# The last quarter of an MLP input product by seven block products instead of eight, on one Trainium2 core

## The reference, cut to what matters

```python
def reference(x, ...):
    h = rms_norm(x, pre_norm_mix)
    y = hybrid_mixer(h, w_in, ..., w_branch_att, w_branch_dn, w_out)
    x = x + rms_norm(y, post_norm_mix)
    h = rms_norm(x, pre_norm_mlp)
    y = jnp.square(jax.nn.relu(h @ w_mlp_in)) @ w_mlp_out    # 1024 x 4096, 4096 x 1024
    x = x + rms_norm(y, post_norm_mlp)
```

## Time and profile before

| | |
|---|---|
| median of 3 runs | 748.72 us (748.64 to 749.12) |
| the profiled execution | 748.65 us |
| its span | 747.1 us |
| TensorE (PE) busy | 739.8 us, 99% |
| VectorE, ScalarE, GpSimd busy | 436.2, 389.3, 317.3 us |
| MLP input stretch, from its first full unit | 424.68 to 588.37 us |
| MLP output stretch | 588.37 to 741.1 us |

### The profile page before, as it was taken

The page is one execution under the profiler, slowest core; times in us unless marked ns, Lnnn a source line. Parts: engine busy times, 40 slices in busy tenths (PEclk is TensorE's granted clock), DMA queues, the critical chain, the costliest instruction groups (busy, mean ns, idle before and its releaser), DMA issues.

```text
span 747.1 us, 11902 instructions
## 1 busy us (share of the span) xinstructions
PE 739.8 (99%) x4168; PEld 608.1 (81%) x4168; DVE 436.2 (58%) x651; ACT 389.3 (52%) x632; POOL 317.3 (42%) x296
## 2 busy tenths in 40 slices
PE   9999999999999999999999999999999999999996
PEld 7788778888887878788888988888888888888885
DVE  5896899990444545345974511221221777778795
ACT  6657842268555365635655733332332655565671
POOL 2357894535444754574526454645645000000002
PEclk9999999999999999999999999999999999999999
DMA  9336223446365577266651279789877476654752
GB/s 341 102 93 205 57 77 108 127 128 184 113 156 157 192 174 204 60 159 204 207 183 29 84 244 290 186 269 282 231 238 212 159 222 197 197 186 153 219 174 113
DMA packets 52893, 129.21 MB, mean 173 GB/s; under 512 B 6096, under 2 KB 6512, under 8 KB 50544
## 3 DMA queue, kind: packets, MB, share of 16 engines
q1 hardware_dynamic: 49120, 109.47, 44.7%
q0 software_dynamic: 3392, 18.88, 13.1%
q10 hardware_dynamic: 336, 0.28, 0.1%
HBM read 126.49 MB, written 39.86 MB: 223 GB/s over the span
## 4 chain that ended last, share of the span: by engine, by line
PE 93%; POOL 3%; ACT 2%; DVE 1%; issue 0%; POOLq 0%; ACTq 0%; DVEq 0%
PE bank L758 28%; PE bank L760 27%; PE bank L759 27%; POOL rsq L2158 2%; PE bank L1005 1%; PE bank L1028 1%; PE bank L1015 1%; POOL w_lo L2164 1%; PE bank L969 1%; PE bank L779 1%; PE bank L933 1%; PE bank L785 1%; PE bank L980 1%; PE bank L1037 1%; PE bank L788 0%; PE bank L1067 0%
## 5 line engine op out<-in xcount | busy, mean ns | idle before, releaser
L2164 POOL TENSOR_TENSOR w_lo<-raw,w_hi 128x512 fp32r<-128x512 f32 x169 | 220.0, 1311 | 238.4 <-ACT w_hi L1220 236.6
L1220 ACT ACTIVATE w_hi<-raw 128x512 fp32r<-128x512 f32 (+2 forms) x214 | 144.9, 684 | 156.3 <-PE bank L760 122.6
L758 PE MATMUL bank<-h_hi,w_hi 128*128 128x512 f32 (+1 forms) x528 | 208.5, 395 | 0.2
L759 PE MATMUL bank<-h_lo,w_hi 128*128 128x512 f32 (+1 forms) x528 | 204.2, 387 | 0.0
L760 PE MATMUL bank<-h_hi,w_lo 128*128 128x512 f32 (+1 forms) x528 | 204.1, 387 | 0.0
L758 PEld LDWEIGHTS bank<-h_hi,w_hi 128*128 128x128 f32 x528 | 99.1, 188 | 25.5 <-issue 5.1
L760 PEld LDWEIGHTS bank<-h_hi,w_lo 128*128 128x128 f32 x528 | 99.2, 188 | 20.6
L759 PEld LDWEIGHTS bank<-h_lo,w_hi 128*128 128x128 f32 x528 | 99.3, 188 | 18.7
L1629 DVE SCALAR_TENSOR_TENSOR relu_sb<-bank,rs_row 128x512 f32<-128x512 f32 x32 | 20.6, 686 | 126.0 <-PE bank L760 114.3
L2305 POOL TENSOR_SCALAR ssh<-ssy 128x1 f32<-128x1 f32 x4 | 1.0, 238 | 151.6 <-ACT junk L1600 151.6
L758 PE MATMUL bank<-w_hi,a_hi 128*128 128x512 f32 x120 | 46.8, 390 | 0.0
(11 more groups left out here) (327 smaller groups left out, 1260.8 us busy)
## 6 DMA issues: line engine op xcount, KB each, us to landing
raw<-in_w_in SPq DMA_DIRECT2D x87, 256.0 KB, 2.7
raw<-in_w_mlp_in SPq DMA_DIRECT2D x62, 256.0 KB, 5.1
t_sum<-in_w_mlp_out POOLq DMA_DIRECT2D x12, 1024.0 KB, 9.0
raw<-in_w_mlp_out SPq DMA_DIRECT2D x26, 256.0 KB, 2.7
raw<-t_sum SPq DMA_DIRECT2D x26, 256.0 KB, 2.9
v_sum<-in_w_mlp_out POOLq DMA_DIRECT2D x4, 1024.0 KB, 9.4
raw_b<-in_w_mlp_out SPq DMA_DIRECT2D x16, 256.0 KB, 2.9
raw_b<-t_sum SPq DMA_DIRECT2D x14, 256.0 KB, 2.9
```

Of the source, the lines that this page charges most:

```text
L758: pe.matmul(o, s_hi, m_hi, start=start, stop=False, skip_group_check=True)
L759: pe.matmul(o, s_hi, m_lo, start=False, stop=False, skip_group_check=True)
L1220: return a.activation(o, i_, ACT.Copy, scale=scale)
L2164: g.tensor_tensor(w_lo[:, slot, :], raw[:, slot, :], w_hi[:, slot, :].bitcast(F32), ALU.subtract).then_inc(lo_ready, 1)
```

## The change

The first 12 groups (G_PLAIN) of the MLP input stay. The last four, 1024 features, become a product of 2 x 2 x 2 blocks: two halves of the tokens (256), of the rows (512) and of the features (512). It is done in 2 steps (STEPS_IN) of 256 features of each half, and a step has seven products, q1, q6, q5, q2, q7, q3, q4, of two units each (PER_STEP = 14), so 28 units in place of 16. A unit of a product has 12 matmuls of 256 columns. q1, q2 and q4 read w_mlp_in, the other four read sums of its blocks, made in DRAM by copy and add in the attention stage (`IN_SUM_AT`).

The other operands are blocks of h or differences of them, `ts_hi` and `ts_lo`; VectorE makes these in groups 4 to 7 (`full_block`, `t_blocks_made`, `t_low`), ScalarE rounds them. Results are put together from three pairs of banks by VectorE (`step_in`: e1, f, c11, c22, c12, c21, then relu), with one copy of q1 by ScalarE (p1).

In the steps loads go through a ring of 8 slots: four new ones, `raw_m`, and the four of `raw`. Low halves are made by GpSimd for 4 units of a step (LOW_POOL) and by VectorE for the other 10.

The sums of w_mlp_out move. Two more pieces, (0,2) and (1,2), are made ahead of the MLP input, at units 114 and 118. `SUM_IN` is left with seven, in groups 2 to 8, and the piece (3,3) goes into the second step. A copy of q = 3 now always waits for all four adds of t2.

As the blocks of h need room, x_res is copied to DRAM in groups 2 and 3 and read back by GpSimd in the MLP output; pn_mlp is loaded there too, in another place. Slots 6 and 7 of the MLP output (`raw_c`) lie at 84 KB in place of 0, so their first load comes before the others' and not after the MLP input.

```diff
-OUT_SUM_AT = {48: 0, 52: 1, 60: 2, 87: 3}
+OUT_SUM_AT = {55: 0, 61: 1, 70: 2, 85: 3}
-SUM_AT = {61: (0, 0), 65: (1, 0), 73: (2, 0), 74: (0, 1), 78: (1, 1), 86: (2, 1)}
+SUM_AT = {64: (0, 0), 73: (1, 0), 76: (2, 0), 79: (0, 1), 82: (1, 1), 88: (2, 1), 114: (0, 2), 118: (1, 2)}
+IN_SUM_AT = {48: (0, 0), 51: (1, 0), 58: (2, 0), 68: (3, 0)}
-SUM_IN = {2: (0, 2), 3: (0, 3), 4: (3, 0), 5: (3, 1), 7: (2, 2), 8: (2, 3), 9: (1, 2), 10: (1, 3), 12: (3, 2), 13: (3, 3)}
+SUM_IN = {2: (0, 3), 3: (1, 3), 4: (2, 2), 5: (2, 3), 6: (3, 0), 7: (3, 1), 8: (3, 2)}
+IN_PRODUCTS = ("q1", "q6", "q5", "q2", "q7", "q3", "q4")
+LOW_POOL = (1, 3, 7, 11)
...
# SP, MLP input
-        for g in range(2, 16):
+        for g in range(2, G_PLAIN):
             for j in range(4):
                 load(0, j, mlp_source(g, j), g * 4 + (U_OUT + j - RAW - 1))
+                if g in (2, 3) and j % 2:
+                    t = 2 * (g - 2) + j // 2
+                    if t == 0:
+                        sp_.wait_ge(*x2_signal(2))
+                        sp_.wait_ge(*x2_signal(3))
+                    sp_.dma_start(x2_copy[t], x_res[:, t, :]).then_inc(copied_out, 16)
             if g in SUM_IN:
                 q, i = SUM_IN[g]
                 if q == 2:
-                    sp_.wait_ge(t_added[0], 16 * N_SUM)
+                    sp_.wait_ge(*added(0, N_SUM))
                 if q == 3:
-                    sp_.wait_ge(t_added[2], 16 * (2 if i < 2 else N_SUM))
+                    sp_.wait_ge(*added(2, N_SUM))
                 sp_.dma_start(*t_copy(q, i)).then_inc(t_copied[q], 16)
+        for s in range(STEPS_IN):
+            for v in range(PER_STEP):
+                u = U_S + PER_STEP * s + v
+                if v >= RING - RAW or s:
+                    sp_.wait_ge(*low_of(u - RING))
+                sp_.dma_start(raw_of(u), in_source(s, v)).then_inc(raw_signal(u)[0], 16)
+                if (s, v) == (1, 0):
+                    sp_.wait_ge(*added(3, 3))
+                    sp_.dma_start(*t_copy(3, 3)).then_inc(t_copied[3], 16)
...
# TensorE, one product of a step (waits for banks left out)
+            for half in range(2):
+                u = U_S + PER_STEP * s + 2 * IN_PRODUCTS.index(name) + half
+                pe.wait_ge(*low_of(u))
+                for kk in range(2):
+                    for e in range(2):
+                        c = slice(kk * 256 + e * P, kk * 256 + e * P + P)
+                        x_ = three(bank[IN_BANK[name] + e][:, 0:256], w_hi[:, u % SPL, c], w_lo[:, u % SPL, c],
+                                   *in_operand(name, 2 * half + kk), name in ("q1", "q6", "q5") and half + kk == 0,
+                                   name in ("q2", "q4", "q3") and half + kk == 2)
+                x_.then_inc(unit_done, 1)
...
# SP, MLP output
-        for s in (4, 5, 0, 1, 2, 3):
+        sp_.wait_ge(unit_done, U_M1 - PER_STEP + 4)
+        for s in (4, 5, 6, 7, 0, 1, 2, 3):
...
# GpSimd, MLP input
-        for u in range(U_OUT + 6, U_M1):
+        def add_sum(q, i):
+            g.wait_ge(*copied(q, i + 1))
+            g.dma_start(*t_add(q, i), accum_op=ALU.add, max_dma_last_dim=8192).then_inc(t_added[q], 16)
+
+        for u in range(U_OUT + 6, U_S):
             split_u(u)
             if (u - U_OUT) % 4 == 1 and (u - U_OUT) // 4 - 1 in SUM_IN:
-                q, i = SUM_IN[(u - U_OUT) // 4 - 1]
-                g.wait_ge(t_copied[q], 16 * (i + 1))
-                g.dma_start(*t_add(q, i), accum_op=ALU.add, max_dma_last_dim=8192).then_inc(t_added[q], 16)
+                add_sum(*SUM_IN[(u - U_OUT) // 4 - 1])
+        for t in range(NT):
+            g.wait_ge(part_done, 24 + 8 * t)
+            g.dma_start(x_res[:, t, :], x2_copy[t]).then_inc(late_in, 16)
+        g.dma_start(pn_mlp[:], post_norm_mlp[0].partition_broadcast(P)).then_inc(late_in, 16)
```

More of the change, by code:

```diff
@@ L1488, in square_group, with mlp_in @@
                              relu_sb[:, 2 * q + m, :].rearrange("p (s c) -> p s c", s=2), ACT.Square).then_inc(act_ready, 1)
[L1490 removed]
+        def mlp_in(i, first, blocks=False):
             for j in range(8):
@@ L1494, in mlp_in @@
                     a.wait_ge(row_full, 1)
-                    mark(copy(rs_row[:], bank[7][:]), row_ready)
+                    mark(copy(rs_row, bank[7][:]), row_ready)
+                    mark(copy(rs_ext[:, 0:256], bank[7][:, 256:512]), row_ready)
                     square_group(i, 0)
[L1497 to L1502, removed]
+                if not (first and j < 3):
@@ L1503, in mlp_in @@
                     split(None, u % 4, i * 32 + 16 * loads(u), i * 8 + (u - 3))
-                if j == 3 and not first or j == 7 and not last:
+                if j == 3 and not first or j == 7:
                     square_group(i, j // 4)
+                if blocks and j in (2, 3, 4, 5):
+                    a.wait_ge(diffs_made, OUT_G + j - 1)
+                    if j == 2:
+                        a.wait_ge(copied_out, 16 * (1 + NT))
+                    b = T_ORDER[j - 2]
+                    copy(ts_hi[b][:], t_full[b][:]).then_inc(dhi_ready, 1)
@@ new lines, in split_in, with mlp_in_last @@
+        def split_in(u):
+            a.wait_ge(*raw_signal(u))
+            a.wait_ge(unit_done, u - 3)
+            copy(w_hi[:, u % 4, :], raw_of(u)).then_inc(hi_ready, 1)
+        def mlp_in_last(i):
+            for j in range(8):
+                u = U_OUT + LEAD + 8 * i + j
+                if u < U_S:
+                    split(None, u % 4, 16 * loads(u), u - 3)
+                else:
+                    split_in(u)
+                if j in (3, 7):
+                    square_group(i, j // 4)
@@ L1517, in _ @@
         mlp_in(0, True)
-        with a.Fori(1, 7) as i:
+        with a.Fori(1, 3) as i:
             mlp_in(i, False)
-        mlp_in(7, False, True)
+        mlp_in(3, False, True)
+        for i in range(4, G_PLAIN // 2 - 1):
+            mlp_in(i, False)
+        mlp_in_last(G_PLAIN // 2 - 1)
+        for s in range(STEPS_IN):
+            mlp_in_step(s)
         def one(i, last=False):
@@ L2038, in _ @@
+        relu(0, True)
+        relu(1, ms=(0, 1))
+        combine(0)
+        relu(1, ms=(2, 3))
+        combine(1)
+        relu(2, ms=(0, 1))
+        combine(2)
+        for b in range(4):
+            full_block(b)
+        relu(2, ms=(2, 3))
+        combine(3)
+        t_blocks_made()
+        relu(3, ms=(0, 1))
+        combine(4)
+        for i in range(4):
+            t_low(i)
+        relu(3, ms=(2, 3))
+        combine(5)
+        for i in range(4, G_PLAIN // 2):
             relu(i, ms=(0, 1))
-            combine(i * 2 - 2)
+            combine(2 * i - 2)
+            if i == G_PLAIN // 2 - 1:
+                for u in range(U_S, U_S + LEAD):
+                    in_low(u)
@@ L2051, in _ @@
         a_low(1, 1, slice(0, 4), 2)
+        for e in range(2):
+            relu_in(STEPS_IN - 1, e)
         w_low(6, 2, 8)
```

306 lines of the change are left out of this document (254 added, 52 removed).

## The result

| | before | after |
|---|---|---|
| median of 6 runs | 748.68 us (748.24 to 749.12) | 757.46 us (755.22 to 759.62) |
| ratio | | 1.0117, 95% interval 1.0093 to 1.0140 |
| the profiled execution | 748.65 us, span 747.1 | 759.15 us, span 757.4 |

The kernel is slower by 1.2%. The forecast was 753.8 us, slower, range 745.3 to 760. The profiled execution is one of the slower of the six (1.7 us over the median), so the amounts read from it are larger than the median's.

The account below looks back on a forecast made before the run. TensorE was taken as the bound, holding 93% of the chain of waits. Matmuls -3.3, stand at unit 28 +6.2, second stand +0.5 and clock +1.7 sum to +5.1 on 748.65: 753.8 us, range 745.3 to 760.

Parts of the forecast that it names:

- Matmuls: MLP input on TensorE: 192 matmuls of 512 columns removed, 336 of 256 columns added, a gain of 3.3 us.
- Helpers in the steps: In the two steps, VectorE's 17.3 of 20.1 us per step, ScalarE, GpSimd and loads fit: 0, up to 3 us.
- The blocks' differences: MLP input: 12 VectorE operations of 1.22 us and 4 ScalarE copies, where VectorE is busy 38 of 164 us: 0.
- Before the MLP input: Attention stage: extra and moved copies and adds, the one behind unit 116 tight: cost 0, at worst 0.5 us for it.
- The stand at unit 28: MLP input: TensorE idles because load 28 queues behind a copy awaiting the add behind unit 25: 6.2 us, bounds 1.9 to 10.1.
- Unit 20 and unit 32: MLP input loads delayed by copy waits: unit 20 costs 0, at worst 1.5 us; unit 32 costs 0.5, range 0 to 2.4.
- Clock: After TensorE's idle stretch the clock falls to half level: 1.7 us, between 0 and about 2.8.
- Rival A: MLP input: the add lands within 6 us, load 28 is in time, no stand, 745.4 us; chance 0.21.
- Rival B: MLP input: about equal, a stand of 1.9 to 4.5 us without a clock fall, 747.3 to 750 us; chance 0.11.
- Rival D: Steps: 256-column matmuls do not run at 0.12 us; at 0.125, +1.7 us; chance 0.11 shared with Rival C.
- part 1: The matmul count for the MLP input: gain 3.3 us from trace rows; the skill's formula would give an estimated 4.7.
- Rival C: Steps: VectorE becomes the bound or the load ring runs dry, +3 to +4 us; chance 0.11 shared with Rival D.

Follow-up runs that it names:

- Experiment 9: Changed kernel: copy (1,3) in group 6, (3,0) to (3,3) in 7 to 10, (0,2)'s add behind unit 119, last step's relu and squares in halves; 747.1 us.
- experiment 4: experiment 1's kernel with the add of (3,3) issued only after 16 parts of the MLP output, not in the second step; 748.07 us.
- experiment 6: experiment 4's kernel with the last step's relu and squares moved, in one piece, behind the work for MLP output parts 8 to 15; 749.41 us.
- experiment 7: Changed kernel with only the last step's relu and squares moved, in one piece, behind the work for MLP output parts 8 to 15; 755.6 us.
- experiment 10: Experiment 9's kernel, but with copy (1,3) in group 3 and the add of (0,2) behind unit 116; 747.04 us.
- experiment 1: Changed kernel with copies (3,0), (3,1), (3,2) in groups 8, 9, 10 in place of 6, 7, 8; 748.9 us.
- experiment 5: Changed kernel with copies (3,0) to (3,3) in groups 7 to 10 and no copy or add in the steps; 749.14 us.
- experiment 2: Kernel before with only the copy order changed: (3,2) in group 9, right behind (2,3), then (1,2), (1,3), (3,3); 750.82 us.
- experiment 3: Changed kernel with copy (1,3) in group 9 in place of 3, and (3,0) left in group 6; 756.24 us.

## Why the prediction was right

The forecast was slower by 5.1 us, and 8.8 were measured, 10.5 in the profiled execution. Direction and main mechanism are as forecast; the sum is short by a stand that it did not have. By its steps:

- **Matmuls, -3.3 us.** Right: the steps take 40.31 us for 336 matmuls, 0.120 each, as the earlier trace rows; the removed ones stood at 0.2267. Experiment 9's span is 2.7 below the old one with the small gaps in it.
- **Helpers in the steps, 0.** Right in the steps, and the terms with it: the 128x256 operations that read a bank took 0.42 us, the lower bound (I took 0.5); VectorE was busy 31.3 of 40.3 us. The part left out was what the last step leaves behind: its relu of two 128x768 and four squares fall into the MLP output, where a round has too little slack on ScalarE for 2.2 us in one piece. That stand, 2.0 us and 1.7 of half clock in the profiled execution, is in none of the sums. Experiments 4, 6, 7, 9 and 10 show it: it moves with the work, and is gone when the work is in halves and the add is not there. The loads beside the add of (3,3) made it longer by 0.8 (experiments 1 and 4).
- **The blocks' differences, 0.** Put at nothing because VectorE is busy 38 of 164 us there. It cost nothing in the changed kernel's trace, but several of these operations took 2.3 us in place of 1.22, beside GpSimd's low halves, and three of the other kernels' traces have the stand at unit 31 of experiment 1. A busy share does not tell whether two engines can work at the same moment.
- **Before the MLP input, 0 to 0.5.** 0.3 at 400.5 us, the place named, behind the add behind unit 116; 0.2 at 387 I had not named. With the add behind 119 the first is gone.
- **The stand at unit 28, 6.2 us (1.9 to 10.1).** 6.7 us. The add was issued at 482.1 (479.5 forecast), landed in 7.7 (8.2), the load in 5.6 (6.0). The chain holds link by link, and experiment 1 takes 8.6 us away with it. The two ends of the range have a meaning: the lower is what the order costs by itself, the rest is the add's lateness and a longer landing, from transfers that are in flight ahead of it. I had put that backlog in from the trace of before, as the same traffic; it was rather more, and group 4 waits 4.1 us for its add (what x_res going out does to it was not tested). That 6.2 came so near 6.7 is partly luck: the same order had 4.3 in the trace of experiment 7.
- **Unit 20 and unit 32.** Unit 20 took no harm; unit 32 stood 0 us in the changed kernel, where I took 0.5. The stands of about 1 us in the traces of kernels with other orders are at other units, 23 and 31, and have the causes told in experiments 5 and 1.
- **Clock, 1.7 us.** 2.2 us behind the stand, plus 1.7 behind the second.
- **Not in the sum at all:** the stand at 606 with its half clock, 3.7 us, and gaps of 1.2 us in all, half of them the three before the MLP input. With them and the measured terms the sum gives the 10.5 of the profiled execution.

Rival A (the add lands in 6 us) is wrong: 7.7, 7.6, 8.0 and 9.6 us in the four traces where SP's queue stood. The Trainium skill's fit (DMA: Bandwidth & Descriptors, Anatomy of one DMA), an estimated 4.4 us for 1 MB, does not hold for this transfer, which reads its destination too. Rival B's stand is that of experiment 2, without the product. Rival D is wrong: the starts are 0.120 apart. (The estimate of 4.7 us for the gain, in the prediction's part 1, comes to 4.8 from its own terms; nothing hangs on it.) Rival C is wrong in the steps, and half right: the work of the steps that is not done in the steps was what it should have looked at.

## What to carry to other kernels

In a queue that is worked through in order, count for each wait how many units later the awaited transfer is *issued* on the other engine, and add its landing; where that is more than the loads behind the wait have to spare, TensorE pays, and three numbers in a table decide more (8.6 us) than the products that were saved (3.3). A backlog ahead of the awaited transfer, which cost nothing in the kernel before, is added to that stand one for one: 1.8 us for the order alone, up to 6.7 under load. When work is cut at a stage's end, look for its leftovers in the next stage, and give them in pieces smaller than one round's slack. And when one engine's work seems to fit into its idle time, look at which other engine works at that moment.

## What the runs showed of the hardware

- A stand of TensorE of 2.0 us at 606 us in the changed kernel was followed by 3.4 us at the half level of the clock, and so was one of 2.0 us at 604 in experiment 3; one of 2.3 us in experiment 1 and one of 1.8 us in experiment 2 were followed by none. Stands of 3.8, 4.3 and 6.7 us all had it, for 3.4, 6.8 and 6.8 us.
- A 1 MB accumulating add landed in 7.6 to 8.0 us with loads beside it for 1.1 us at most (changed kernel, experiments 2 and 3), and in 9.6 with two loads still in flight for its first 2.6 us (experiment 7). 256 KB loads that lay beside such adds for nine tenths of their time or more took 2.6 to 11.6 us in the changed kernel, the middle one 9.0, against 2.5 to 2.7 with no other transfer in flight (four loads of the changed kernel and the kernel before).
- VectorE's operations with both inputs and the result in SBUF were held up beside GpSimd's low halves: in experiment 1 one of 128x256 took 5.87 us in place of 0.41 while GpSimd made four, and ended 0.3 us behind the last; those of 128x1024 took 2.2 to 2.3 us in place of 1.22 there, and the low halves 2.2 in place of 1.3. In TensorE's and ScalarE's rows of the same time nothing is longer.
- The changed kernel's executions scatter by 4.4 us, the kernel before's by 0.9. The cause is not shown; experiments 9 and 10, without the long waits, still scatter by 3.4.
